# A mixture-of-experts decoder step on one core: two or four experts share a 128-row job, and results are summed to tokens on chip

## What is computed

```python
def moe_ffn(h, router_w, router_bias, e_gate, e_up, e_down, s_gate, s_up, s_down):
    ...
    w = w / jnp.sum(w, axis=-1, keepdims=True) * ROUTED_SCALE
    gates = jnp.zeros((n, N_EXPERTS), jnp.float32).at[jnp.arange(n)[:, None], idx].set(w)
    hg = jnp.einsum('nd,edf->nef', h, e_gate)
    hu = jnp.einsum('nd,edf->nef', h, e_up)
    act = jax.nn.silu(hg) * hu * gates[:, :, None].astype(h.dtype)
    routed = jnp.einsum('nef,efd->nd', act, e_down)
    shared = (jax.nn.silu(h @ s_gate) * (h @ s_up)) @ s_down
    return routed + shared
```

## Time and profile before

| what | us |
|---|---|
| median of 3 runs | 1030.38 |
| range of the runs | 1030.37 to 1033.02 |
| profiled execution, its time | 1032.84 |
| its span, first to last instruction | 1031.0 |
| TensorE busy | 935.5 (91%) |
| VectorE busy | 474.9 (46%) |
| ScalarE busy | 282.5 (27%) |
| GpSimd busy | 174.7 (17%) |

### The profile page before, as it was taken

How to read it: one execution, slowest core, us unless ns; L and a number is a source line. 1 busy time by engine, 2 the same in 40 slices (tenths; PEclk the granted TensorE clock), 3 DMA queues, 4 the chain that set the end, 5 groups by cost and what they waited for, 6 DMA issues and landing times.

```text
span 1031.0 us, 18438 instructions
## 1 busy us (share of the span) xinstructions
PE 935.5 (91%) x6425; PEld 652.6 (63%) x6425; DVE 474.9 (46%) x1210; ACT 282.5 (27%) x501; POOL 174.7 (17%) x173
## 2 busy tenths in 40 slices
PE   2799999999999988999999999999989979979870
PEld 1699999999997866445555555555545445445430
DVE  1656889899857443622233222332322222222117
ACT  3544344434373120111212212121212111111122
POOL 2000000000000001022223223322222222221222
PEclk9899999999999969999999999999999989999995
DMA  9975558777766185479999999999999999999833
GB/s 334 261 236 163 169 166 295 236 262 285 230 243 234 40 339 219 177 289 330 400 396 400 401 408 397 395 396 400 384 382 350 360 358 348 364 354 343 322 78 110
DMA packets 103497, 305.58 MB, mean 296 GB/s; under 512 B 13251, under 2 KB 55363, under 8 KB 78452
## 3 DMA queue, kind: packets, MB, share of 16 engines
q1 hardware_dynamic: 89715, 283.80, 73.2%
q0 software_dynamic: 13232, 19.68, 8.0%
q10 hardware_dynamic: 499, 1.40, 0.4%
HBM read 304.78 MB, written 26.97 MB: 322 GB/s over the span
## 4 chain that ended last, share of the span: by engine, by line
PE 73%; DMA 19%; DVE 5%; ACT 1%; issue 1%; SPq 0%; ACTq 0%; DVEq 0%; POOLq 0%
PE psum L755 25%; DMA wexp<-in_e_up 17%; PE psum L1022 14%; PE psum L1024 8%; PE psum L759 7%; PE psum L1055 5%; PE psum L1050 4%; PE psum L774 2%; PE psum L1025 2%; PE psum L945 2%; DMA bc<-in_norm_g 1%; PE psum L810 1%; PE psum L936 1%; PE psum L993 1%; PE psum L973 1%
## 5 line engine op out<-in xcount | busy, mean ns | idle before, releaser
L755 PE MATMUL psum<-xn_r,wexp_r 128*128 128x264 f32 x1024 | 191.4, 287 | 2.2 <-DVE wexp_r L1436 2.2
L1024 PE MATMUL psum<-wexp,mid 128*64 128x256 f32 x720 | 173.9, 384 | 1.0 <-DMA wexp<-in_e_up 0.8
L1025 PE MATMUL psum<-wexp,mid 128*64 128x256 f32 x720 | 174.0, 385 | 0.0
L1022 PE MATMUL psum<-wexp,mid 128*128 128x512 f32 x304 | 148.3, 634 | 22.7 <-DMA wexp<-in_e_up 21.9
L755 PEld LDWEIGHTS psum<-xn_r,wexp_r 128*128 128x128 f32 x1024 | 160.0, 189 | 4.9 <-DVE wexp_r L1436 2.7
L1840 DVE SCALAR_TENSOR_TENSOR hT<-psum,gcol,hT 128x256 f32<-128x256 f32 (+1 forms) x64 | 30.6, 478 | 285.7 <-ACT hT L1347 237.1
L755 PE MATMUL psum<-hT_r,wexp_r 128*128 128x264 f32 x512 | 145.4, 284 | 0.0
L1436 DVE TENSOR_TENSOR wexp_r<-wexp,wexp_r 128x1024 fp32r<-128x1024 f32 x88 | 106.7, 1221 | 25.4 <-ACT wexp_r L1189 25.2
L1024 PEld LDWEIGHTS psum<-wexp,mid 128*64 128x64 f32 x720 | 92.2, 136 | 39.6 <-issue 6.2
L1022 PEld LDWEIGHTS psum<-wexp,mid 128*128 128x128 f32 x304 | 58.7, 203 | 84.0 <-issue 82.8
L1189 ACT ACTIVATE wexp_r<-wexp 128x1024 fp32r<-128x1024 f32 x88 | 92.1, 1053 | 49.9 <-PE psum L755 42.5
(11 more groups left out here) (287 smaller groups left out, 1121.7 us busy)
## 6 DMA issues: line engine op xcount, KB each, us to landing
wexp<-in_e_gate SPq DMA_DIRECT2D x64, 1024.0 KB
wexp<-in_e_up SPq DMA_DIRECT2D x64, 1024.0 KB
wexp<-in_e_down SPq DMA_DIRECT2D x64, 1024.0 KB
wexp<-in_w_in SPq DMA_DIRECT2D x32, 1024.0 KB, 6.3
mid<-in_ada_w SPq DMA_DIRECT2D x8, 2048.0 KB, 9.5
wexp<-in_ada_w SPq DMA_DIRECT2D x4, 2048.0 KB, 20.1
wexp<-in_w_branch SPq DMA_DIRECT2D x8, 1024.0 KB, 5.1
wexp<-in_w_out SPq DMA_DIRECT2D x4, 1024.0 KB, 6.0
```

The source lines that it names most:

```text
L755: last = mm(out, a[x], b[y], start=start and x == y == 0, stop=stop and x == 1)
L1022: last = mm(psum[:, j % 2, :].rearrange("p (a f) -> p a f", a=2), x[:, k, :], w[:, k], start=(k == 0), stop=(k == KT - 1))
L1024: mm(psum[HALF:CAP, j % 2, 0:FE], x[:, k, 0:HALF], w[:, k, 0], start=(k == 0), stop=(k == KT - 1), tile_position=(0, HALF))
L1025: last = mm(psum[0:HALF, j % 2, 0:FE], x[:, k, 0:HALF], w[:, k, 1], start=(k == 0), stop=(k == KT - 1), tile_position=(0, 0))
```

## The change

The jobs no longer have one expert each. There are 33: four fixed ones with one expert as before, then seven rounds of four jobs with 4, 1, 1 and 2 experts (`SHARE`), and a last job of four. All have 128 rows: of an expert that shares with three others up to 32 rows are taken, with one other up to 64. A sorted list of places gives the experts with fewest rows to the jobs of four, the largest to the jobs of one. In a shared job each expert's rows stand at their own 32 or 64 partitions, and `up` and `down` run each expert's weights on its own column tile. A job of four uses all four rooms, the single ones rooms 0 and 1, the job of two rooms 2 and 3. A shared job is finished within its own step: its activation is turned and its down done right behind its up.

The results are no longer scattered. ScalarE rounds them to fp32r (`y_high`), VectorE takes the remainder (`y_low`), and TensorE multiplies both with a one-hot matrix from rows to tokens (`spread_hot`), in five pieces a job: two tiles of 128 tokens times two halves of 512 columns, and the 8 samples. VectorE adds each piece from PSUM to `y_sum` in SBUF. The tables `y_even` and `y_odd`, their zeroing, the scatters and the loads at the end are gone. The shared expert's result goes into the same sums.

```diff
+BODIES = 7
+LAST = BODIES + 1
+N_JOBS = UNROLL * LAST + 1
+PER_BODY = 8
+SHARE = (4, 1, 1, 2)
...
+        def rooms_of(i, j):
+            if isinstance(i, int) and i == 0:
+                return [j]
+            return ([0, 1, 2, 3], [0], [1], [2, 3])[j]
...
+            def jobs_before(i, j, room):
+                if j:
+                    return UNROLL * i + 1
+                if isinstance(i, int) and i == 1:
+                    return room + 1
+                return UNROLL * i - 2 + min(room, 2)
+            def gate_up_of(i, j):
+                for place, room in zip(places_of(i, j), rooms_of(i, j)):
+                    e = expert_at(place)
+                    sp.wait_ge(S["up_done"], jobs_before(i, j, room))
+                    load_gate_up(e, room)
...
+            def body(i):
+                gate_up_of(i, 0)
+                down_of(i, 0)
+                gate_up_of(i, 1)
+                gate_up_of(i, 2)
+                down_of(i, 1)
+                gate_up_of(i, 3)
+                down_of(i, 2)
+                down_of(i, 3)
...
                 for k in ks:
-                    if is_large(i, j):
-                        last = mm(psum[:, j % 2, :].rearrange("p (a f) -> p a f", a=2), x[:, k, :], w[:, k], start=(k == 0), stop=(k == KT - 1))
-                    else:
-                        mm(psum[HALF:CAP, j % 2, 0:FE], x[:, k, 0:HALF], w[:, k, 0], start=(k == 0), stop=(k == KT - 1), tile_position=(0, HALF))
-                        last = mm(psum[0:HALF, j % 2, 0:FE], x[:, k, 0:HALF], w[:, k, 1], start=(k == 0), stop=(k == KT - 1), tile_position=(0, 0))
+                    for q, room, rows, tile in parts_of(i, j):
+                        last = mm(psum[rows, j % 2, :].rearrange("p (a f) -> p a f", a=2), x[:, k, rows], w_gu[room][:, k],
+                                  start=(k == 0), stop=(k == KT - 1), **tile)
...
+            def sum_piece(hot, m):
+                t, h, bank = piece_of(m)
+                t0, n = TILES[t]
+                if t < 2:
+                    for y in (y_high, y_low):
+                        last = mm(psum[:, bank, :], as_r(hot[:, t0:t0 + n]), as_r(y[:, h * BLK:(h + 1) * BLK]), start=(y is y_high), stop=(y is y_low))
+                    return last
+                for y in (y_high, y_low):
+                    for h in range(2):
+                        last = mm(psum[32 * h:32 * h + n, bank, :], as_r(hot[:, t0:t0 + n]).bitcast(F32), as_r(y[:, h * BLK:(h + 1) * BLK]).bitcast(F32),
+                                  start=(y is y_high), stop=(y is y_low), tile_position=(0, 32 * h))
+                return last
+            def sums(i, j, pieces):
+                e = UNROLL * i + j
+                for m in pieces:
+                    if m == 0:
+                        pe.wait_ge(S["hot_ready"], e + 1)
+                        pe.wait_ge(S["y_lo_rows"], 2 * e + 2)
+                    else:
+                        need(pe, S["sum_done"], N_PIECES * e + m - 1)
+                    sum_piece(spread_hot[:, j % 2], m).then_inc(S["sum_full"], 1)
...
+            def body(i):
+                for j in steps(i):
+                    first = isinstance(i, int) and i == 0 and j == 0
+                    summed, waiting = left_over(i, j)
+                    up(i, j, (0, 1))
+                    if summed:
+                        sums(*summed, (0, 1))
+                    up(i, j, (2, 3))
+                    if waiting:
...
+                        turn_act(*waiting)
...
+                    if is_shared(i, j):
+                        turn_act(i, j)
+                        if waiting:
+                            sums(*waiting, range(N_PIECES))
+                        down(i, j)
...
+            def sums_out(i, j):
+                e = UNROLL * i + j
+                need(ve, S["sum_done"], N_PIECES * e)
+                for m in range(N_PIECES):
+                    ve.wait_ge(S["sum_full"], N_PIECES * e + m + 1)
+                    add_piece(m, S["sum_done"])
...
             def y_out(i, j):
                 e = UNROLL * i + j
-                ve.wait_ge(S["down_done"], 2 * e + 2)
-                need(ve, scattered[j % 2], 16 * (2 * i + j // 2))
-                n = rows_used(i, j)
-                V.tensor_copy(y_rows[0:n, j % 2, BLK:2 * BLK], psum[0:n, 4, :]).then_inc(S["ys_dve"], 1)
+                for h in range(2):
+                    a = slice(h * BLK, (h + 1) * BLK)
+                    ve.wait_ge(S["y_hi_rows"], 2 * e + h + 1)
+                    V.tensor_tensor(as_r(y_low[:, a]), psum[:, 3 + h, :], as_r(y_high[:, a]).bitcast(F32), ALU.subtract).then_inc(S["y_lo_rows"], 1)
```

More of the change, by code:

```diff
@@ L683, in _ @@
             pool.wait_ge(S["x2_ready"], 6)
             g.dma_start(fing, final_g.rearrange("(a d) -> a d", a=1).to_broadcast([P, D])).then_inc(S["ld_fin"], 16)
-            def body(i, first=False, last=False):
-                for j in range(UNROLL):
-                    if not (first and j == 0):
-                        scatter(i if j else i - 1, (j - 1) % UNROLL)
-                    if not last:
+            def body(i):
+                for j in steps(i):
+                    if follows(i + 1, j):
@@ L1072, in sort, with body @@
                 mm(psum[:, 2, 3 * P:3 * P + NE], expert[:, :], to_job[:, 0, :], start=True, stop=True).then_inc(S["sort_out"], 1)
[L1074 to L1080 removed]
+            def body(i):
+                for j in steps(i):
+                    first = isinstance(i, int) and i == 0 and j == 0
[5 more added lines that the diff above has]
+                    if waiting:
+                        if isinstance(i, int) and i == 0 and j == 1:
@@ L1081, in body @@
                             pe.wait_ge(S["job_ready"], 1)
-                        turn_act(pi, pj)
-                    else:
+                        turn_act(*waiting)
+                    if first:
                         turn_for_sort()
-                    up(i, j, (4, 5, 6, 7))
-                    if not (last and j == UNROLL - 1):
-                        turn_rows(i if j < 3 else i + 1, (j + 1) % UNROLL)
-                    if prev:
-                        down(pi, pj)
-                    else:
+                    if summed:
+                        sums(*summed, (2, 3))
@@ L1091, in body @@
+                    up(i, j, (4, 5))
+                    if summed:
+                        sums(*summed, (4,))
+                    up(i, j, (6, 7))
+                    if not (isinstance(i, int) and i == LAST):
+                        turn_rows(*one_after(i, j))
+                    if waiting:
+                        down(*waiting)
+                    if first:
                         sort()
                         shared_down()
-                    if not last:
+                    if follows(i + 1, j):
@@ L1103, in _ @@
-            turn_act(NE // UNROLL - 1, UNROLL - 1)
-            down(NE // UNROLL - 1, UNROLL - 1)
+            body(BODIES)
+            body(LAST)
+            sums(LAST, 0, range(N_PIECES))
             def extra(r, e, n):
@@ L1354, in y_out @@
[L1354 to L1366 removed]
+                need(ac, S["sum_full"], N_PIECES * e)
@@ L1878, in sort_out, with body @@
                 ve.wait_ge(S["job_ready"], 1)
-            def body(i, first=False, last=False):
-                for j in range(UNROLL):
-                    prev = not (first and j == 0)
-                    pi, pj = (i if j else i - 1), (j - 1) % UNROLL
-                    if not prev:
+            def body(i):
+                for j in steps(i):
+                    first = isinstance(i, int) and i == 0 and j == 0
+                    summed, waiting = left_over(i, j)
+                    if summed:
+                        sums_out(*summed)
+                    if first:
```

482 lines of the change are left out of this document (247 added, 235 removed).

## The result

The changed kernel takes 1039.2 us (median of 4 runs, 1036.74 to 1041.49) against 1031.7 us for the one before on the same chip: 1.0075 times the time, with an interval of 1.0051 to 1.01. It is slower by 7.5 us where 1015.1 us, 15 us faster, was forecast. The time lies inside the range; the sign was wrong.

A forecast was written before the change was run, and what follows sets the result against it. TensorE was to bound the rounds: 64.5 us of work plus 5.8 of waits made 70.3 each; with opening, last job and a 17.3 us tail the span was 1015.7, the median 1015.1 us, range 998 to 1045.

The forecast's parts named there:

- the transfer term: Loads and gathered rows of a round of eight experts: 65.5 us at 400 GB/s, under TensorE's 70.3.
- the late slow rate: Late rounds of the kernel before: their 359 GB/s was said to come with the scatters.
- The slow rival: In the rounds, transfers set the pace: 74 to 75 us a round, about 1045 us in all; chance 0.18.
- the far bound: Upper end of the eight-in-ten range for the whole kernel, 1045 us.
- the list: Token-list products on TensorE, growing from 12 to 24 of three columns' worth: 0.7 us a round.
- Work without waits: TensorE's round: jobs 47.2, sums 14.4, lists 0.7 and tile changes 2.2, together 64.5 us.
- terms 1 and 2: Job of four: waits for VectorE's gating, 0.8 us, and for the copy of the turned activations, 0.6 us.
- (4): Between the two single jobs: VectorE's gating and copy of turned rows stand bare, 0.8 us.
- (5): Split of rows in high and low before the sums, short where the job of two carries them: 0.8 us.
- (6): Five sum pieces in a row on two banks, each emptied by a slower add: 0.8 us.
- (7): The down behind the five pieces waits for the last add: 0.7 us.
- Term (3): First single job's weights, issued only when the job of four frees its rooms: 7.9 against 6.6 us, wait 1.3.

The follow-up runs named there:

- without the sums: The changed kernel with the products that sum rows to tokens and their adds left out; 968.26 us in one execution.
- order changed: The changed kernel with, in the job of four, one-hots made before VectorE's fifth add and the activation turned before the token list; 1031.41 us, ratio 0.9992.
- loop written out: The changed kernel with TensorE's loop over rounds 2 to 6 unrolled, so the list's places are constants; 1028.88 us, ratio 0.9969.
- filling the gap: The changed kernel with four unread 128-column products added between the job of four's turned activation and its down; 1029.55 us, ratio 0.9983.
- after: The changed kernel itself as first profiled, against the kernel before; median 1039.2 us, ratio 1.0075, profiled execution 1036.74 us.
- list behind the down: The changed kernel with the job of four's twelve token-list products moved to follow its own down; 1031.97 us, ratio 0.9996.
- two pieces in the gap with the loop written out: Changed kernel with fp32r samples, reordered one-hots and turn, two sum pieces behind the job of four's up, and TensorE's loop unrolled; 998.15 us, ratio 0.9652.
- samples' piece in fp32r: The changed kernel with the samples' sums as two whole-array fp32r pieces instead of fp32 on two tiles; 1014.28 us, ratio 0.9826.
- samples and order: The changed kernel with whole-array fp32r samples' sums, plus earlier one-hots and the activation turned before the list; 1002.06 us, ratio 0.9704.

## Why the forecast was wrong, by its own steps

**What sets the pace: right.** TensorE bounds the rounds, the transfer term holds (65.5 forecast, 64.4 to 66.2 without the sums), and the late slow rate came with the scatters. The slow rival, transfers set the pace, is refuted, although the time came out on its side. That the time lies inside the range is owed to the far bound, which was drawn for that rival.

**The work of a round: the list is the term that was mis-sized.** The up of four with its sums takes 11.2 us (558.07 to 569.30 with the order changed) as worked out, so an up on four column tiles costs what was said, and a job's sums too. But the twelve-product list was costed by its columns, like the short lists of before. In the loop its places come from registers, and it takes 1.63 us against 0.45: 1.2 us a round that no row of before could show in this size. The registers alone do not do it, since without the sums, or behind the down, the same list takes 0.45 in the loop. The five pieces in a row take 4.4 us (620.35 to 626.17 with the order changed, less 1.4 idle) where 3.6 was worked out. Work without waits is 66.5 us in the undisturbed round (71.2 less 4.65 idle), not 64.5.

**The waits: right in kind, too large in sum.** The releasers are those of the list: in a looped round 0.45 and 1.06 in the gap (terms 1 and 2), 0.78 on the row copy (4), 0.94 on the split (5), 0.43 and 0.19 on the banks (6), 0.79 before the down (7). That is 4.6 us, against 5.8. Term (3), the first weights, is 0 in the loop: the longer list and the slow down cover the 7.7 us from the end of the up of four to the weights, near the 7.9 of the forecast, and it comes back as 1.3 where the list is short (last round, and the loop written out). Other executions show up to 9.3.

**The clock: the step that failed.** The forecast said that the idle stretches which drew the clock to 0.95 would go, and its list of signs has a clock of 1.00. It gave the clock no term in the sum when it added waits of its own. The downs of four show 0, 2.5, 1.6, 2.8, 1.7 and 0 us over 3.64, 8.6 us in all, 1.4 a round (11.9 in all when the kernel ran again); filling the gap gave 8.0 us back. The first up of the rounds lost another 1.5.

So a round is 70.3 + 1.4 (clock) + 1.2 (list) + 0.8 (other work, the five pieces above all) − 1.2 (waits) = 72.5, as measured. That is also the round at which the forecast expected no change.

**The ends.** What makes it slower than before is the beginning: the first round takes 81.2 instead of 77.6. Of the 3.6 us, 1.5 are the clock at 0.50 in its first quarter of an up (3.41 us against 1.92); its waits are 6.6 instead of 5.8 (1.03 of them for the load of 498.50, forecast at 1.3), and its work 73.1 instead of 71.8. The stretch ahead of it is 1.1 us longer than forecast, with the wait for all four rooms in it, 3.14 where 3.4 was forecast. The first up starts 1.1 us later, which is no effect of the change: between executions it starts from 404.0 to 406.7 us. The part behind the last up of four takes 23.4 instead of 22.0. The tail is 16.1 us where 17.3 was forecast, and 32.2 before, so the gain there is real. In sum 1.1 + 1.1 + 3.6 + 13.2 + 1.4 − 1.2 = 19.2 us, from 1015.7 to the span of 1034.9. The medians are 24.1 us apart (1015.1 and 1039.2): the profiled execution of before lay 2.5 us above its median, and this one 2.5 below. When the kernel ran again, a profiled execution of 1037.9 us began its first up 2.4 us earlier and had rounds of 73.0 on the mean, so the clock may well take more in the median than in the rows here; the slower executions of the first four were not profiled.

The margin was the weak point: a gain of 15 us against seven rounds, each allowed to be off by 2.2 us. The bounds of 64.5 to 76 were stated, but the 0.70 for "faster" read the middle as if its errors were independent, when all of them lie in the same repeated round.

## What to carry to other kernels

When an edit puts waits into a loop in which TensorE was busy throughout, cost the clock as well: turns and products of few columns did not hold it up here, and a stretch of them and of waits made the dense block behind it slow. Fill such a gap with work that has to be done anyway (here pieces of the sums), and put short products with addresses from registers behind a long block. When halved work gives nothing back, look at the form of what was added: the samples' piece in fp32 on two tiles rather than in fp32r on the whole array cost 23 us.

## What the runs showed of the hardware

- The granted clock falls from 1.00 to 0.50 and is back at 1.00 some 3 to 7 us later. What went before: 1.5 us of bare waits and 1.6 us of 6-column products (after); those products and turns with 0.34 us bare (order changed); 0.72 and 1.03 us of waits around two turns (list behind the down). In the loop written out it did not fall behind 0.33 and 0.55 us with a 0.46 us list, nor behind the 1.3 to 2.7 us of waiting for weights that follow a full down of 3.64 us.
- A full down of 3.64 us in front does not protect the clock: it fell behind waits for weights of 2.2 to 2.6 us (two pieces in the gap with the loop written out), 2.6 (samples' piece in fp32r, last round) and 3.5 us (order changed, last round), and held behind 2.1 (list behind the down, last round), 2.3 (samples and order, last round) and 2.7 us.
- The same sequence keeps the clock in one round and loses it in the next (after 576 and 648 us; samples and order 705 and 772 us), and in the same round in one execution and not in another (the first looped one of after and of its second run). What decides between them stays open. The Trainium skill (TensorEngine Tiling (Array Packing), PSUM Bottleneck) warns of the emptying of PSUM in such a kernel; here it showed as the short waits on `L1898`, 0.2 to 0.8 us each in a looped round, not as VectorE being the bound (555.4 us busy of 1034.9).
- Twelve 6-column products with addresses from registers take 1.63 to 1.81 us where the up in front is cut up by sums, 1.11 to 1.24 behind 1.2 us of sums and two turns, 0.46 behind a down of over 3.6 us, 0.44 to 0.45 behind an up without sums and the turned rows, and 0.45 with constant addresses.
- Once the rooms come free together, the queue stands empty (0 GB/s at 716 us) and then runs at some 380 to 475 GB/s in windows of a microsecond.
